# Norm gains of k and q moved into the rope tables, reciprocal roots into ScalarE's k copy and the exponential's scale

## What is computed

```python
h = rms_norm(x, norm_g[l])
proj = einsum('bsd,de->bse', h, w_in[l])          # u, v, z of branch a; q, k, v, z of branch b; index q, k, w; two gates
q = apply_rope(rms_norm(b_q.reshape(b, s, 4, 128), q_norm_g[l]), cos_q, sin_q)
k = apply_rope(rms_norm(b_k.reshape(b, s, 4, 128), k_norm_g[l]), cos_q, sin_q)
att = sparse_attention_branch(q, k, v, qi, ki, i_w, topk)   # an indexer picks 128 keys; softmax over att * 128 ** -0.5
```

## Time and profile before

| | us |
|---|---|
| median of 3 runs (lowest, highest) | 787.42 (785.97, 787.47) |
| profiled execution, its own time | 785.83 |
| its span, first to last instruction | 784.0 |
| TensorE busy | 770.4 |
| VectorE busy | 626.3 |
| ScalarE busy | 427.5 |
| GpSimd busy | 169.6 |

### The profile page before, as it was taken

How to read it: one execution, slowest core, us unless ns; L and a number is a source line. 1 busy time by engine, 2 the same in 40 slices (tenths; PEclk the granted TensorE clock), 3 DMA queues, 4 the chain that set the end, 5 groups by cost and what they waited for, 6 DMA issues and landing times.

```text
span 784.0 us, 12204 instructions
## 1 busy us (share of the span) xinstructions
PE 770.4 (98%) x4412; PEld 675.8 (86%) x4412; DVE 626.3 (80%) x1050; ACT 427.5 (55%) x790; POOL 169.6 (22%) x151
## 2 busy tenths in 40 slices
PE   7999999999989999999999999999999999999998
PEld 7988888888889889988899888888888998999886
DVE  5779999978788685679986798999787868746895
ACT  6566656341577347734564775643335773566342
POOL 1257511100130103012211674020012201110130
PEclk9999999999999999999999999999999999999999
DMA  9634237743877338685873532478158953577684
GB/s 331 225 115 127 82 108 158 159 115 85 157 123 211 70 82 141 194 237 117 191 237 108 163 84 79 135 147 202 55 104 158 170 161 58 111 140 229 163 147 123
DMA packets 54541, 113.67 MB, mean 145 GB/s; under 512 B 3536, under 2 KB 8848, under 8 KB 54480
## 3 DMA queue, kind: packets, MB, share of 16 engines
q0 software_dynamic: 22960, 47.27, 32.6%
q1 hardware_dynamic: 31232, 65.02, 25.7%
q10 hardware_dynamic: 288, 0.59, 0.2%
HBM read 97.14 MB, written 6.29 MB: 132 GB/s over the span
## 4 chain that ended last, share of the span: by engine, by line
PE 86%; DVE 8%; DMA 2%; issue 2%; ACT 1%; SPq 0%; DVEq 0%; ACTq 0%
PE bank L858 15%; PE bank L860 15%; PE bank L859 15%; PE bank L926 5%; PE bank L928 5%; PE bank L927 5%; PE bank L979 4%; PE bank L895 3%; PE bank L897 3%; PE bank L896 3%; PE bank L832 2%; DVE w_lo L1425 2%; PE bank L850 2%; PE bank L788 1%; DMA x_sb<-in_x 1%
## 5 line engine op out<-in xcount | busy, mean ns | idle before, releaser
L1425 DVE TENSOR_TENSOR w_lo<-w_raw,w_hi 128x1024 fp32r<-128x1024 f32 x156 | 201.4, 1302 | 13.9 <-ACT w_hi L1064 9.1
L1064 ACT ACTIVATE w_hi<-w_raw 128x1024 fp32r<-128x1024 f32 x156 | 160.4, 1052 | 22.5 <-DMA w_raw<-in_w_out 15.6
L858 PE MATMUL bank<-w_lo,h_hi 128*128 128x512 f32 x256 | 100.5, 393 | 0.0
L860 PE MATMUL bank<-w_hi,h_hi 128*128 128x512 f32 x256 | 99.9, 390 | 0.0
L859 PE MATMUL bank<-w_hi,h_lo 128*128 128x512 f32 x256 | 99.8, 390 | 0.0
L732 POOL DMA_DIRECT2D w_raw<-in_w_in x32 | 38.6, 1207 | 246.1 <-DVE w_lo L1425 246.1
L926 PE MATMUL bank<-h_hi,w_lo 128*128 128x256 f32 x256 | 75.8, 296 | 1.8 <-DVEq L1581 1.8
L858 PE MATMUL bank<-h_lo,w_hi 128*128 128x512 f32 x192 | 75.3, 392 | 0.0
L860 PE MATMUL bank<-h_hi,w_hi 128*128 128x512 f32 x192 | 74.8, 389 | 0.0
L859 PE MATMUL bank<-h_hi,w_lo 128*128 128x512 f32 x192 | 74.7, 389 | 0.0
L928 PE MATMUL bank<-h_hi,w_hi 128*128 128x256 f32 x256 | 72.4, 283 | 0.0
(11 more groups left out here) (208 smaller groups left out, 1857.6 us busy)
## 6 DMA issues: line engine op xcount, KB each, us to landing
w_raw<-in_w_in SPq DMA_DIRECT2D x88, 512.0 KB, 4.4
w_raw<-in_w_in POOLq DMA_DIRECT2D x32, 512.0 KB, 5.9
w_raw<-in_w_out POOLq DMA_DIRECT2D x16, 512.0 KB, 6.4
w_raw<-in_w_out SPq DMA_DIRECT2D x12, 512.0 KB, 4.0
out<-x_sb POOLq DMA_DIRECT2D x4, 1024.0 KB, 5.5
w_raw<-in_w_oa SPq DMA_DIRECT2D x8, 512.0 KB, 3.6
w_raw<-in_w_ob SPq DMA_DIRECT2D x8, 512.0 KB, 4.2
x_sb<-out POOLq DMA_DIRECT2D x2, 2048.0 KB, 10.1
```

Source lines behind the costliest of these rows:

```text
L858: nc.tensor.matmul(dst, s_h, m_l, start=(n == 0), stop=False)
L860: last = nc.tensor.matmul(dst, s_h, m_h, start=False, stop=(n == len(pairs) - 1))
L1064: nc.scalar.activation(hi, w_raw[:, raw_slot(layer, u)], ACT.Copy).then_inc(s_whi.sem, 1)
L1425: nc.vector.tensor_tensor(lo, w_raw[:, raw_slot(layer, u)], hi.bitcast(F32), ALU.subtract) \
```

## The change

The gains are multiplied into rope tables once per layer: `rope_g` holds, for k and q and each token tile, cosines and sines of 128 columns times the gain. GpSimd makes it with four products after the third index tile. For this the stash of x tiles 2 and 3 is issued before the second index tile, since `rope_g` lies in the memory of `v_b`; the `v_b` copies wait until the rotations that read `rope_g` are done. GpSimd's two products per tile go, its cosine product reads `rope_g`. The reciprocal roots of k are applied by ScalarE, whose copy to `stage` becomes four copies with a scale column each, after the reciprocal and after what else ScalarE does for the job. q is staged without its root; the root (with the attention scale in it, by a second `eps` column and scale in the Sqrt) is the scale of the exponential and of `neg_max`. VectorE's reciprocal waits for the root (`s_std`) instead of the staged tile. FILL becomes smaller in size, so that its product with a root stays finite.

```diff
-FILL = -(2.0 ** 126)
+FILL = -(2.0 ** 116)
...
+        with ExitStack() as early:
+            rope_g = sb("rope_g", [P, 2, TILES, 2, DH], keep=early)
         v_b = sb("v_b", [P, TILES, HEADS * DH])
...
+        def q_scale(i):
+
+            h, b = ATT_STEPS[i]
+            c = HEADS * (TILES + b) + h
+            return rstd[:, c:c + 1]
...
+                def gains_in_tables():
+
+                    pool.wait_ge(s_stash2.sem, s_stash2.at(layer, 16))
+                    for i, g_bc in enumerate((kg_bc, qg_bc)):
+                        gain = g_bc[:].rearrange("p (s d) -> p s d", s=2).unsqueeze(1).to_broadcast([P, TILES, 2, DH // 2])
+                        for j, table in enumerate((cq, sq)):
+                            poo.mark(nc.gpsimd.tensor_tensor(
+                                rope_g[:, i, :, j].rearrange("p t (s d) -> p t s d", s=2),
+                                table.unsqueeze(2).to_broadcast([P, TILES, 2, DH // 2]), gain, ALU.mult))
+                    poo.join(pool)
+                    pool.sem_inc(s_table.sem, 1)
...
                 for n in range(TILES):
+                    if n == 1:
+                        pool.wait_ge(s_xn.sem, s_xn.at(layer, TILES))
+                        pool.dma_start(stash[:, 2:4], x_sb[:, 2:4]).then_inc(s_stash2.sem, 16)
...
                     times_cos(n, stage[:, n % 2, first * ID:ROT_I], IH + 1 - first, ID, ci[:, b])
+                    if n == 2:
+                        gains_in_tables()
                 for n in range(2 * TILES):
-                    g_bc = kg_bc if n < TILES else qg_bc
-                    tile = stage[:, (TILES + n) % 2, 0:HEADS * DH].rearrange("p (h d) -> p h d", h=HEADS)
-                    pool.wait_ge(s_rinv.sem, s_rinv.at(layer, n + 1))
-                    poo.link(pool, nc.gpsimd.tensor_tensor(
-                        tile, tile, rstd[:, HEADS * n:HEADS * n + HEADS].unsqueeze(2).to_broadcast([P, HEADS, DH]),
-                        ALU.mult))
-                    nc.gpsimd.tensor_tensor(tile, tile, g_bc[:].unsqueeze(1).to_broadcast([P, HEADS, DH]),
-                                            ALU.mult).then_inc(s_xg.sem, 1)
-                    pool.wait_ge(s_xg.sem, s_xg.at(layer, n + 1))
-                    times_cos(TILES + n, stage[:, (TILES + n) % 2, 0:HEADS * DH], HEADS, DH, cq[:, n % TILES])
-                    if n == 0:
-                        pool.dma_start(stash[:, 2:4], x_sb[:, 2:4]).then_inc(s_stash2.sem, 16)
+                    pool.wait_ge(s_stage.sem, s_stage.at(layer, TILES + n + 1))
+                    times_cos_gains(TILES + n, n)
...
-                act_.mark(root(layer, std[:, c:c + HEADS], ms[:, c:c + HEADS]))
+                if n < TILES:
+                    op = root(layer, std[:, c:c + HEADS], ms[:, c:c + HEADS])
+                else:
+                    op = nc.scalar.activation(std[:, c:c + HEADS], ms[:, c:c + HEADS], ACT.Sqrt, bias=eps[:, 1:2],
+                                              scale=ATT_SCALE ** -2)
+                op.then_inc(s_std.sem, 1)
...
                     head_std(layer, t, src)
+                    if n in JOB_K:
+                        return
...
-                    if t == 0:
-                        act.wait_ge(s_stash2.sem, s_stash2.at(layer, 16))
+                    act.wait_ge(s_rot.sem, s_rot.at(layer, (2 if t < 2 else 3) * TILES))
                     act_.mark(nc.scalar.activation(v_b[:, t], src[:], ACT.Copy))
...
+            def k_staged(layer, n):
+
+                t = n - JOB_K[0]
+                src, free = bank[bank_of(n)], s_free[bank_of(n)]
+                act.wait_ge(s_rinv.sem, s_rinv.at(layer, t + 1))
+                for h in range(HEADS):
+                    cols = slice(h * DH, (h + 1) * DH)
+                    act_.mark(nc.scalar.activation(stage[:, (TILES + t) % 2, cols], src[:, cols], ACT.Copy,
+                                                   scale=rstd[:, HEADS * t + h:HEADS * t + h + 1]))
+                act_.join(act)
+                act.sem_inc(free.sem, 1)
+                act.sem_inc(s_stage.sem, 1)
...
-                                                       bias=neg_max[:, i:i + 1], scale=ATT_SCALE,
+                                                       bias=neg_max[:, i:i + 1], scale=q_scale(i),
...
                     beside(layer, n)
+                    if n in JOB_K:
+                        k_staged(layer, n)
...
-                    dve.wait_ge(s_xg.sem, s_xg.at(layer, m + 1))
-                    rotate(layer, n, rot[:, 0:HEADS * DH], stage[:, n % 2], HEADS, DH, sq[:, m % TILES]).then_inc(s_rot.sem, 1)
+                    dve.wait_ge(s_stage.sem, s_stage.at(layer, n + 1))
+                    dve.wait_ge(s_table.sem, s_table.at(layer, 1))
+                    sine = rope_g[:, m // TILES, m % TILES, 1]
+                    rotate(layer, n, rot[:, 0:HEADS * DH], stage[:, n % 2], HEADS, DH,
+                           (sine[:, DH // 2:DH], sine[:, 0:DH // 2])).then_inc(s_rot.sem, 1)
...
-                nc.vector.tensor_scalar(neg_max[:, i:i + 1], row_max[:, i:i + 1], -ATT_SCALE, None,
+                dve.wait_ge(s_rinv.sem, s_rinv.at(layer, 2 * TILES))
+                nc.vector.tensor_scalar(neg_max[:, i:i + 1], row_max[:, i:i + 1], q_scale(i), -1.0, ALU.mult,
                                         ALU.mult).then_inc(s_max.sem, 1)
...
-                    dve.wait_ge(s_stage.sem, s_stage.at(layer, TILES + m + 1))
+                    dve.wait_ge(s_std.sem, s_std.at(layer, m + 1))
                     nc.vector.reciprocal(rstd[:, c:c + HEADS], std[:, c:c + HEADS]).then_inc(s_rinv.sem, 1)
```

More of the change, by code:

```diff
@@ L332, in trunk @@
         gate_half = sb("gate_half", [P, 2 * KD])
-        eps = sb("eps", [P, 1])
+        eps = sb("eps", [P, 2])
         head_w = sb("head_w", [P, TILES, IH])
@@ L386, in trunk @@
         s_stage = sig("tile_staged", 3 * TILES)
-        s_xg = sig("heads_scaled", 2 * TILES)
+        s_std = sig("heads_std", 2 * TILES)
+        s_table = sig("rope_tables_with_gains", 1)
         s_cos = sig("tile_times_cos", 3 * TILES)
@@ L643, in _ @@
         def _(pool):
-            seed(pool, s_xg, s_cos)
+            seed(pool, s_cos, s_table)
             def small_weights(layer):
@@ L683, in times_cos, with times_cos_gains @@
                         cos.unsqueeze(1).to_broadcast([P, 2 * heads, dim // 2]), ALU.mult).then_inc(s_cos.sem, 1)
+                def gains_in_tables():
[8 more added lines that the diff above has]
+                    pool.sem_inc(s_table.sem, 1)
+                def times_cos_gains(n, m):
+                    pool.wait_ge(s_rot.sem, s_rot.at(layer, n))
+                    nc.gpsimd.tensor_tensor(
+                        rope_a[:, 0:HEADS * DH].rearrange("p (h d) -> p h d", h=HEADS),
+                        stage[:, n % 2, 0:HEADS * DH].rearrange("p (h d) -> p h d", h=HEADS),
+                        rope_g[:, m // TILES, m % TILES, 0].unsqueeze(1).to_broadcast([P, HEADS, DH]),
+                        ALU.mult).then_inc(s_cos.sem, 1)
                 for n in range(TILES):
+                    if n == 1:
+                        pool.wait_ge(s_xn.sem, s_xn.at(layer, TILES))
+                        pool.dma_start(stash[:, 2:4], x_sb[:, 2:4]).then_inc(s_stash2.sem, 16)
                     pool.wait_ge(s_stage.sem, s_stage.at(layer, n + 1))
@@ L1052, in _ @@
             act.dma_start(norm_bc[:], norm_g[0]).then_inc(s_norm0, 16)
-            seed(act, s_whi, s_shi, s_xstd, s_hhi, s_small, s_stage, s_rotc, s_relu, s_va, s_u, s_wsc,
+            seed(act, s_whi, s_shi, s_xstd, s_hhi, s_small, s_std, s_stage, s_rotc, s_relu, s_va, s_u, s_wsc,
                  s_lnstd, s_tanh, s_yahi, s_ga, s_gb, s_mhi, s_exp, s_ptc, s_ybhi, s_bhi, s_s5hi, s_shi3, s_asnap, s_bsnap, s_hshi, s_prob, s_hpart, *s_free.values())
@@ L1090, in root @@
             def root(layer, dst, src, scale=1.0):
-                return nc.scalar.activation(dst, src, ACT.Sqrt, bias=eps[:], scale=scale)
+                return nc.scalar.activation(dst, src, ACT.Sqrt, bias=eps[:, 0:1], scale=scale)
             def head_std(layer, n, src):
@@ L1412, in _ @@
             vec.mark(nc.vector.memset(diag[0:CHUNK, CHUNK:P], FILL))
-            vec.mark(nc.vector.memset(eps[:], EPS))
+            vec.mark(nc.vector.memset(eps[:, 0:1], EPS))
+            vec.mark(nc.vector.memset(eps[:, 1:2], EPS * ATT_SCALE ** -2))
             vec.join(dve)
@@ L1426, in remainder, with rotate @@
                     .then_inc(s_wlo.sem, 1)
-            def rotate(layer, n, dst, tile, heads, dim, sin):
+            def rotate(layer, n, dst, tile, heads, dim, sines):
                 w, half = heads * dim, dim // 2
@@ L1432, in rotate @@
                 b = rope_b[:, 0:w].rearrange("p (h d) -> p h d", h=heads)
-                first, second, sine = slice(0, half), slice(half, dim), sin.unsqueeze(1).to_broadcast([P, heads, half])
```

(8 more changed lines are left out.)

## The result

The changed kernel takes 788.45 us (median of 9 runs, 787.81 to 789.84), the kernel before in the same rounds 786.78 us (9 runs). The ratio is 1.0024, with an interval of 1.0014 to 1.0034: slower by 0.24%, 1.7 us by the medians and 1.9 by the ratio. The prediction held that up to 0.2% can't be told from no change; the measured value lies just above that bound, the interval on both sides of it, and all of it above 1. The profiled execution took 788.03 us with a span of 786.2, 2.2 more than before, at the same granted clock of 0.998.

A forecast was written before the change was run, and what follows sets the result against it. TensorE was taken to bound the kernel, with VectorE's queue late before gate a. Three parts at 0 and the attention step's +0.96 us on the median 787.42 gave 788.3 us, range 785.8 to 790.2.

The forecast's parts named there:

- What bounds the kernel: TensorE, busy 770.4 of 784.0 us and full in 64 to 90 us; one real hole a layer, 2.25 and 2.26 us.
- parts 1 to 3: GpSimd's removed products, tables with earlier stash, and ScalarE scaling k: value 0 each; the first at best -4.5 us.
- the 23 us that the prediction named: VectorE time that could come back: 12 us at w_lo subtractions, 11 us at first halves of rotations.
- the forecast of 28 us net: GpSimd's loss in both layers: 40.4 us of products removed, 10 to 13 us of table products added.
- Part 4, the step's price: Attention step's column operands: exponential +0.10 us, neg_max +0.06, further wait 0; 0.16 us longer a step.
- Part 4, the count: Three attention steps a layer on the chain, two layers: 6 x 0.16 = +0.96 us, bounds 0 and 1.3.
- The forecast stalls: TensorE's three stalls before gate a's products, 220 to 246 us: each some 0.16 us longer, 2.7 us in all.
- All hidden: In the attention step, operand reads overlap with what goes before: +0, 787.4 us; chance 0.22.
- Relief reaches the end: VectorE enters the gate stage less late, holes close: 4.5 us gives 782.9, half of it 785.2; chance 0.11.
- ScalarE held in the k stage: Late reciprocal holds ScalarE's queue, rotated k tiles miss transposition: 794.0 us, or 791.2 at one tile a layer; chance 0.15.

The follow-up runs named there:

- the kernel with one wait a layer: Changed kernel with VectorE's wait for the reciprocals before neg_max made only at each layer's first attention step: 787.20 us, ratio 1.0022 to the kernel before.
- the first run: Kernel before with only exponential and neg_max of every attention step reading the attention scale from an SBUF column, not a constant: 788.04 us, ratio 1.0024.
- the second: Changed kernel with constants again in exponential and neg_max, q's roots applied by ScalarE's four copies like k's: 785.77 us, ratio 1.0001 to the kernel before.
- moved rounds: Top-k rounds of jobs 31, 33, 35 go to 23 and 30, of 46 to 45: kernel before 782.35 us (0.9954), changed kernel 783.62 us (0.9968).
- the three with one VectorE instruction more: Kernel before with a scale column in the exponential, in neg_max, or in both, filled by one added VectorE instruction: 787.67, 787.48 and 788.04 us.

## Why the prediction was right, and where it was not

**The figure.** 788.3 us was forecast, 788.45 measured, within the range. But it was forecast as "within 0.2%", on its slower side, and it is 0.24%: the term of the sum was too small, +0.96 us where the ratio measures +1.9, interval 1.1 to 2.7. That the two times agree so well is luck: the median of the kernel before was 787.42 us then and 786.78 beside the result, and from the latter the same sum gives 787.7. (787.42 + 0.96 is also 788.4 and not 788.3.)

**What bounds the kernel, and parts 1 to 3.** Right. Their value of 0 is measured within 0.1%, not only argued: 1.0001 with all three in place, and stalls as before. TensorE is full in 64 to 90 us, w_lo's mean is 1.234 us (1.24 was forecast), the eight table products take 1.3 us each. The rule of the Trainium skill, SBUF — State Buffer, "Who interferes with whom", that a VectorE instruction with two SBUF inputs and a GpSimd instruction that reads SBUF exclude each other, agrees with the durations: with most of GpSimd's products gone VectorE got back 21.4 of the 23 us that the prediction named, and 7.8 at two indexer's products that it did not name. GpSimd gained as well, which the forecast of 28 us net left out: its cosine products fell from 1.61 to 1.29 us each, and it lost 36.0 us. ScalarE's four copies of a k tile take 1.15 us together (9.2 us for 32), not 1.3. They were worth nothing: VectorE's idle time grew, and no work on TensorE's path moved forward.

**Part 4, the step's price.** Right: 0.093 + 0.060 = 0.153 us against 0.16, and 0 for the wait, as taken. That the bias column is there already hides nothing of the second one. The Trainium skill, ScalarE: Activation LUTs, "What ACT_TABLE_LOAD costs", has some 93 ns for each `[128,1]` pointer operand; the rows before and after, 723 and 816 ns, agree for a second operand.

**Part 4, the count.** Here is the mis-sized term: "Three steps a layer lie on the chain, two layers: 6 x 0.16", and behind it "The other 26 steps lengthen too, but TensorE does not wait there". It does at step 9, where two more steps add up with no slack in front of them. Five steps a layer give 10 x 0.153 = 1.5 us; the kernel with only the columns measures 1.9, interval 1.0 to 2.7, and 0.35 of that is in its trace the place at 568 us, which is not the columns'. The changed kernel's trace does not have that place; beyond the five steps it has 0.36 us at 274 us, an idle time of VectorE of 0.71 us instead of 0.35 before step 9 begins, which the kernel with one wait a layer does not have. The prediction listed the holes of TensorE, and step 9 was none: it was a start with 0.05 us of slack.

**The forecast stalls.** "Each some 0.16 us longer, 2.7 us in all": 0.16, 0.11 and 0.14, 2.67 in all.

**The rivals.** All hidden: refuted by the first run. Relief reaches the end: refuted by the second, in both layers. ScalarE held in the k stage: refuted by the same run, which holds it for eight more tiles; in the changed kernel the 32 copies wait 1.0 us in all. In the gate stage, with moved rounds, ScalarE's queue seems to become the bound, which none of the rivals foresaw.

**Open.** What makes the idle times of 0.36 us that come and go with the instruction list; why the changed kernel with moved rounds loses 0.2 us more in layer 1 than in layer 0; how much of layer 0's gain from moved rounds most executions keep; and whether the exponential of step 3, put ahead of the gate's work on ScalarE, closes the stall that is left. No run here settles any of these.

## What to carry to other kernels

Before counting what a slightly longer instruction costs, list every place where the bottleneck engine starts on a result that has been ready for less than the time you add (here 0.05 us, with 0.3 us added by two steps), not only where it waits: no view of waits shows a place without slack. Work taken off an engine is worth what the bottleneck waits for it, here 26 us for nothing, while three rounds of 1.4 us taken out of one queue in each layer gave 0.5%. Scalars moved into operands to save a pass are paid for in every instruction that reads them, and in a round trip between two engines both prices add.

## What the runs showed of the hardware that was not expected

- A second column operand costs the exponential 0.089 to 0.093 us at 128 to 512 columns, about what the first costs in the earlier trace rows (0.10). On VectorE a column in place of a constant costs 0.060 us even for one element a partition (0.154 to 0.214 us).
- Idle times without a releaser, or longer than their releaser explains, come in a size of 0.35 to 0.36 us and at places that differ from one instruction list to the next: at 554 us 3.11 us in the kernel before, 3.47, 3.46 and 3.47 in the three with one VectorE instruction more, 3.12 in the changed kernel and in the one with its step undone, 2.76 in the changed kernel with one wait. One such place is worth 0.05% of this kernel, a fifth of the change's whole effect.
- VectorE's instruction of 8 elements a partition, `head_w`, took 1.01 and 0.99 us beside a table product of GpSimd, once a layer (at 40 and 425 us), and 0.16 to 0.18 at its six other places.
- One and the same weight DMA of 512 KB took 6.1, 7.1 and 8.0 us to land in three traced executions, in which it was issued at 378.4, 376.8 and 376.6 us.
